# A mixer's turns by DMA, sums in parts, memory rows earlier, and a first weight unit in two

## What is computed

```python
# first block, layer l                      # second block, layer l
x += 0.5*rms_norm(swiglu(rms_norm(x)))      x += rms_norm(parallel_mixer(rms_norm(x)))
x += rms_norm(hybrid_mixer(rms_norm(x)))    x += rms_norm(memory_cross_attention(rms_norm(x), rms_norm(mem)))
x += 0.5*rms_norm(swiglu(rms_norm(x)))      x += rms_norm(swiglu(rms_norm(x)))
```

## Time and profile before

| | |
|---|---|
| median of 3 runs | 2045.92 us (2045.69 to 2047.0) |
| the profiled execution | 2046.49 us, span 2044.6 us |
| TensorE busy | 2022.4 us, 99% |
| VectorE busy | 1411.0 us, 69% |
| ScalarE busy | 1122.0 us, 55% |
| granted TensorE clock, in tenths | 9 (90% or more) in all 40 slices |
| DMA | 389.31 MB, mean 190 GB/s |

### The profile page before, as it was taken

One profiled execution on the slowest core, in us unless ns is written; L12 is line 12 of the kernel. 1 busy time (PEld: TensorE's weight loads), 2 busy tenths in 40 slices (PEclk: granted clock), 3 DMA queues, 4 the chain that ended last, 5 costly groups with the idle time before them and its releaser, 6 DMA issues.

```text
span 2044.6 us, 24517 instructions
## 1 busy us (share of the span) xinstructions
PE 2022.4 (99%) x9754; PEld 1669.8 (82%) x9754; DVE 1411.0 (69%) x1855; ACT 1122.0 (55%) x1414; POOL 0.2 (0%) x4
## 2 busy tenths in 40 slices
PE   7999999999999999999999999999999999999998
PEld 6888887888888888887878888898888888988887
DVE  6656898776667566998776566856756668567565
ACT  5445657564446445667564446656644566565443
POOL 0000000000000000000000000000000000000000
PEclk9999999999999999999999999999999999999999
DMA  8766764557766775664567766444677664446764
GB/s 269 213 209 182 220 202 144 174 192 208 216 205 211 206 216 181 211 191 150 178 212 223 202 189 203 153 150 141 188 209 214 186 201 145 159 140 186 210 212 119
DMA packets 330226, 389.31 MB, mean 190 GB/s; under 512 B 102640, under 2 KB 238464, under 8 KB 330112
## 3 DMA queue, kind: packets, MB, share of 16 engines
q1 hardware_dynamic: 326016, 376.70, 60.7%
q10 hardware_dynamic: 4096, 11.05, 1.5%
HBM read 365.66 MB, written 1.05 MB: 179 GB/s over the span
## 4 chain that ended last, share of the span: by engine, by line
PE 91%; DVE 4%; ACT 2%; DMA 2%; issue 1%; SPq 0%; DVEq 0%; ACTq 0%
PE ps L585 82%; PE ps L1086 2%; DVE w_lo L1827 1%; DMA raw<-in_ffn_w_up 1%; DVE scratch L2092 1%; PE ps L653 1%; ACT w_hi L1249 1%; PE ps L1189 1%; PE ps L1170 1%; PE ps L676 1%; PE ps L822 1%; DVE x L1867 0%; DMA raw<-in_w_in 0%; PE ps L1034 0%; PE ps L728 0%
## 5 line engine op out<-in xcount | busy, mean ns | idle before, releaser
L1827 DVE TENSOR_TENSOR w_lo<-raw,w_hi 128x2048 fp32r<-128x2048 f32 x338 | 772.5, 2289 | 268.1 <-ACT w_hi L1249 265.6
L1249 ACT ACTIVATE w_hi<-raw 128x2048 fp32r<-128x2048 f32 x342 | 648.2, 1898 | 461.5 <-PE ps L585 261.2
L585 PE MATMUL ps<-w_hi,hT_hi 128*128 128x512 f32 x2048 | 807.1, 394 | 2.0 <-DVE w_lo L1827 2.0
L585 PE MATMUL ps<-w_lo,hT_hi 128*128 128x512 f32 x2048 | 798.4, 390 | 0.0
L585 PE MATMUL ps<-w_hi,hT_lo 128*128 128x512 f32 x2048 | 775.4, 390 | 0.0
L585 PEld LDWEIGHTS ps<-w_hi,hT_hi 128*128 128x128 f32 x2048 | 385.0, 188 | 85.9 <-issue 5.5
L585 PEld LDWEIGHTS ps<-w_hi,hT_lo 128*128 128x128 f32 x2048 | 383.6, 188 | 79.8
L585 PEld LDWEIGHTS ps<-w_lo,hT_hi 128*128 128x128 f32 x2048 | 385.3, 188 | 77.1
L585 PE MATMUL ps<-w_hi,bT_hi 128*128 128x512 f32 x592 | 232.3, 392 | 1.6 <-DVE bT_lo L1908 1.5
L585 PE MATMUL ps<-w_hi,bT_lo 128*128 128x512 f32 x592 | 230.5, 389 | 0.0
L585 PE MATMUL ps<-w_lo,bT_hi 128*128 128x512 f32 x592 | 230.5, 389 | 0.0
(11 more groups left out here) (292 smaller groups left out, 1283.3 us busy)
## 6 DMA issues: line engine op xcount, KB each, us to landing
raw<-in_w_in SPq DMA_DIRECT2D x160, 512.0 KB, 4.6
raw<-in_ffn_w_gate SPq DMA_DIRECT2D x88, 512.0 KB, 4.0
raw<-in_ffn_w_up SPq DMA_DIRECT2D x88, 512.0 KB, 5.0
raw<-in_ffn_w_down SPq DMA_DIRECT2D x88, 512.0 KB, 4.3
raw<-in_w_gate SPq DMA_DIRECT2D x44, 512.0 KB, 4.0
raw<-in_w_up SPq DMA_DIRECT2D x44, 512.0 KB, 5.0
raw<-in_w_down SPq DMA_DIRECT2D x44, 512.0 KB, 4.3
raw<-in_w_out SPq DMA_DIRECT2D x32, 512.0 KB, 4.4
```

The lines of the kernel that those rows point to most:

```text
L585: mm = nc.tensor.matmul(bank(t, half), act[:, tiles[i], t * P:(t + 1) * P], w, start=start and (i, n) == steps[0], stop=stop and (i, n) == ...
L1249: nc.scalar.activation(dst, src, ACT.Copy).then_inc(high_ready, 1)
L1827: V.tensor_tensor(lo, src, flat(hi), ALU.subtract).then_inc(low_ready, 1)
```

## The change

- The second mixer's q, k and lru inputs are parted, turned by DMA from SP's queue behind units 9, 10 and 11, and joined; `fox_turn`, `lru_turn` and two copies go, q's factor 1/8 moves into its row scale, `fox_decay` comes after unit 5.
- `sb_sums` takes the softplus rows as a high and a low fp32r part, which VectorE makes; the ones stay in float32. One merge moves ahead of the softplus.
- In `first_pair` the two row turns of x's second half stand together; ScalarE copies the weight unit after the last turned tiles.
- The memory rows are loaded and normalised during the last layer's first feed-forward of the first block, in memory of their own.
- The first unit is loaded, copied and subtracted in two halves; the gains are loaded ahead of the identity and x.

```diff
@@ -299,6 +301,10 @@
     lxy = pairbuf.rearrange("p (t n) -> p t n", t=TT)
+    fq_planes, fq_planes_T = planes(wide[:, 0:1024]), planes_T(rT_f)
+    fk_planes, fk_planes_T = (w.rearrange("p m n -> p (m n)") for w in (vm[:, 0:1, :], vm[:, 1:2, :]))
+    fk_planes, fk_planes_T = planes(fk_planes), planes_T(fk_planes_T)
+    lxy_planes, lxy_planes_T = fq_planes, fq_planes_T
     ry_f, rsq_f = pairbuf[:, 0:512], pairbuf[:, 512:1024]
...
@@ -313,7 +319,8 @@
-    mem_rows, mem_g, mem_sq = merged, conv_y_f, pairbuf
+    mem_rows, mem_g = a_mem(2048).rearrange("p (t n) -> p t n", t=TT), a_mem(1024)
+    mem_sq = out_a
     positions = ctx.enter_context(nc.sbuf_tensor("positions", [P, TT], I32))[:, :]
...
@@ -409,6 +422,11 @@
             u = L.unit(k)
+            if u == 0:
+                for i in range(2):
+                    for dst, src in halves:
+                        sp.dma_start(dst[:, 2 * i:2 * i + 2, :], src[:, 2 * i:2 * i + 2, :]).then_inc(first_landed[i], 16)
+                return
             if u == 1:
...
@@ -529,6 +547,15 @@
                     k += 1
+                    if k == 10:
+                        sp.wait_ge(*after("fox_join", "q_planes", l))
+                        turn_planes(fq_planes_T, fq_planes, fox_q_turned)
+                    if k == 11:
+                        sp.wait_ge(*after("fox_join", "k_planes", l))
+                        turn_planes(fk_planes_T, fk_planes, fox_k_turned)
+                    if k == 12:
+                        sp.wait_ge(*after("lru_turn", "planes", l))
+                        turn_planes(lxy_planes_T, lxy_planes, lru_turned)
                     if (n, kh) == (0, 1):
...
@@ -619,17 +646,18 @@
                         norm_turn(L, j, 0, 1)
-                    if L.sub0 + j and (n, t, i) == (1, 0, 0):
-                        norm_turn(L, j, 1, 0)
+                    if L.sub0 + j and (n, t, i) == (1, 0, 2):
+                        for kh in range(2):
+                            norm_turn(L, j, 1, kh)
                     if n and i == 0:
                         bank_free(t)
+                    if L.sub0 + j == 0 and (n, t, i) == (0, 0, 2):
+                        weights(L, k)
                     pe.wait_ge(hT_hi_ready, L.sub(j, 16, 8 * t + firsts[n] + i + 1))
...
                 def wait(t, i):
-                    if L.sub0 + j and (n, t, i) == (1, 0, 0):
-                        norm_turn(L, j, 1, 1)
                     if i == 0:
...
@@ -639,7 +667,9 @@
             for t, n in order:
-                if t == 0:
+                if t == 0 and L.sub0 + j == 0 and n == 0:
+                    pe.wait_ge(first_low, 1)
+                elif t == 0:
                     weights(L, k + n)
...
@@ -811,16 +841,21 @@
-            pe.wait_ge(*after("sb_keep", f"softplus{c}", l))
+            pe.wait_ge(*after("sb_keep", f"softplus_high{c}", l))
             if c:
...
             for e in range(2):
-                s = sb_sp[:, e * 384:(e + 1) * 384]
-                nc.tensor.matmul(ps[:, 6 + e, 0:384], konst("tri_ge"), s, start=True, stop=False)
-                mm = nc.tensor.matmul(ps[:, 6 + e, P:256], konst("ones"), s[:, 256:384], start=False, stop=True)
+                nc.tensor.matmul(ps[:, 6 + e, 0:384], sb_tri[:, :], sp_hi[:, e * 384:(e + 1) * 384], start=True, stop=False)
+            for e in range(2):
+                nc.tensor.matmul(ps[:, 6 + e, P:256], konst("ones"), sb_sp[:, e * 384 + 256:(e + 1) * 384], start=False,
+                                 stop=False)
+            for e in range(2):
+                pe.wait_ge(*after("sb_keep", f"softplus_low{e}_{c}", l))
+                mm = nc.tensor.matmul(ps[:, 6 + e, 0:384], sb_tri[:, :], sp_lo[:, e * 384:(e + 1) * 384], start=False,
+                                      stop=True)
             mm.then_inc(*done("sb_sums", f"sums{c}"))
...
@@ -967,23 +1002,12 @@
-        def fox_turn(l, which):
-            pe.wait_ge(*after("fox_in", which, l))
-            if which == "k":
-                pe.wait_ge(*after("fox_gate", "rows", l))
-            turn(fq if which == "q" else fk, 4 if which == "q" else 6).then_inc(*done("fox_turned", which))
-
-        def lru_turn(l):
-            pe.wait_ge(*after("lru_in", "xy", l))
-            pe.wait_ge(*after("fox_in", "qT", l))
-            turn(lxy, 4).then_inc(*done("lru_turned", "xy"))
-
         def fox_logits(l, g):
...
             if g == 0:
-                pe.wait_ge(*after("fox_in", "kT", l))
+                pe.wait_ge(*after("fox_join", "k", l))
                 pe.wait_ge(*after("fox_gate", "rows", l))
...
@@ -1094,8 +1118,7 @@
                     ("ret_in", "g"), ("memory_in", "v0"), ("memory_in", "v1")]
-            steps = {(1, 0): [fox_forget], (1, 1): [fox_decay, lambda l: fox_turn(l, "q")],
-                     (2, 1): [lambda l: fox_turn(l, "k")], (3, 1): [lru_turn, lambda l: fox_logits(l, 0)],
+            steps = {(1, 0): [fox_forget], (2, 0): [fox_decay], (3, 1): [lambda l: fox_logits(l, 0)],
                      (4, 1): [lru_gates, lambda l: fox_logits(l, 1)], (5, 0): [lambda l: fox_turn_p(l, 0)],
...
@@ -1242,11 +1265,17 @@
             slot = u % RAW_RING
-            act.wait_ge(raw_landed[slot], (u // RAW_RING + 1) * 32)
+            act.wait_ge(raw_landed[slot], (u // RAW_RING + (slot > 0)) * 32)
             if u >= HIGH_RING:
...
             nc.scalar.activation(dst, src, ACT.Copy).then_inc(high_ready, 1)
+
+        def first_unit_high(i):
+
+            act.wait_ge(first_landed[i], 32)
+            s = slice(1024 * i, 1024 * i + 1024)
+            nc.scalar.activation(w_hi[:, 0, s], raw[:, 0, s], ACT.Copy).then_inc(high_ready if i else first_high, 1)
...
@@ -1319,8 +1348,8 @@
             turned(L, j + 1, 1, 0)
+            turned(L, j + 1, 1, 1)
             high(L, last + PAST)
-            turned(L, j + 1, 1, 1)
...
@@ -1361,7 +1388,11 @@
             for c in range(2, NCHUNK - 1):
+                if memory_here(L, n) and c == 3:
+                    memory_load()
                 chunk(L, k0 + 3 * c - 1, c)
+                if memory_here(L, n) and c == 6:
+                    memory_std(L.l)
             end, c = k0 + U_FFN - 1, NCHUNK - 1
...
@@ -1656,8 +1685,6 @@
             between = {0: lambda: (fox_soft(l), lru_lambda(l)),
-                       2: lambda: (act.wait_ge(*after("fox_turned", "q", l)), copy(fqT, two(4), "fox_in", "qT", 64 ** -0.5)),
-                       3: lambda: (act.wait_ge(*after("fox_turned", "k", l)), copy(fkT, two(6), "fox_in", "kT")),
                        4: lambda: fox_exp(l, 0)}
...
@@ -1676,6 +1703,10 @@
                 dst, stage, step = evicted[n]
+                if n == 0:
+                    act.wait_ge(*after("fox_join", "eighth", l))
+                if n == 4:
+                    act.wait_ge(*after("fox_join", "q", l))
                 rows(dst, chunk_rows(n) if n < 5 else chunk_rows(n)[:, :, 0:256], stage, step)
...
@@ -1773,22 +1804,24 @@
         enter(Layer("A", 0))
-        act.dma_start(const[:, 0:P], d["const"][:, 0:P]).then_inc(ident_loaded, 16)
         rows_of_gains = d["gains"].rearrange("s g (k p) -> (s g k) p", p=P)
-        act.dma_start(x[:, 0, :], d["x"][0, 0:P, :]).then_inc(x_loaded[0], 16)
         for b, (r, end) in enumerate(((0, P), (P, GAIN_ROWS))):
             act.dma_start(gain_rows[0:end - r, b, :], rows_of_gains[r:end, :]).then_inc(gains_loaded, 16)
+        act.dma_start(const[:, 0:P], d["const"][:, 0:P]).then_inc(ident_loaded, 16)
+        act.dma_start(x[:, 0, :], d["x"][0, 0:P, :]).then_inc(x_loaded[0], 16)
         act.dma_start(x[:, 1, :], d["x"][0, P:T, :]).then_inc(x_loaded[1], 16)
...
         act.dma_start(const[:, at:at + width], d["const"][:, at:at + width]).then_inc(const_loaded, 16)
-        high(Layer("A", 0), 0)
+        first_unit_high(0)
         act.wait_ge(gains_ready, 1)
...
                 turned(Layer("A", 0), 0, t, kh)
+                if (t, kh) == (0, 0):
+                    first_unit_high(1)
         for k in range(2, AHEAD + 1):
...
@@ -1825,6 +1858,16 @@
             V.tensor_tensor(lo, src, flat(hi), ALU.subtract).then_inc(low_ready, 1)
+
+        def first_unit_low(i):
+
+            if i:
+                dve.wait_ge(high_ready, 1)
+            else:
+                dve.wait_ge(first_high, 1)
+            s = slice(1024 * i, 1024 * i + 1024)
+            V.tensor_tensor(w_lo[:, 0, s], raw[:, 0, s], flat(w_hi[:, 0, s]), ALU.subtract).then_inc(
+                low_ready if i else first_low, 1)
...
@@ -2127,6 +2173,13 @@
             V.scalar_tensor_tensor(sb_sp, sb_z, 0.0, sb_e, ALU.max, ALU.add).then_inc(*done("sb_keep", f"softplus{c}"))
+            dve.wait_ge(*after("sb_keep", f"softplus{c}", l))
+            V.tensor_copy(sp_hi[:, :], sb_sp).then_inc(*done("sb_keep", f"softplus_high{c}"))
+            dve.wait_ge(*after("sb_keep", f"softplus_high{c}", l))
+            for e in range(2):
+                s = slice(e * 384, (e + 1) * 384)
```

(59 more changed lines are left out.)

15 lines of the change are left out of this document (10 added, 5 removed).

## The result

The changed kernel takes 2033.85 us (median of 6 runs, 2033.39 to 2034.47); the kernel before took 2045.74 us in the runs beside them. The ratio is 0.9943, with an interval of 0.993 to 0.9955: 11.9 us less. The forecast was 2033.0. The sum behind it is less right than the number: one term of it failed by 3.2 us, and others came out larger than predicted.

A forecast was written before the change was run, and what follows sets the result against it. TensorE, busy 99% of the span, was taken to bound the kernel. Terms 5.5 + 3.9 + 0.2 + 1.6 + 2.1 = 13.3 us turned the 2045.92 us median into 2032.6; the forecast was 2033.0, range 2029 to 2040.

The forecast's parts named there:

- second mixer: Turning q, k and lru inputs by DMA takes 48 transposes off TensorE over two layers: net 5.5 us.
- sums in parts: In `sb_sums`, fp32r parts make each call 0.62 us cheaper, call 0 only 0.1: 3.9 us, bounds 2.0 to 4.5.
- merged turns: Two row turns of 4 become one of 8 in 11 places, with no wait there: 0.2 us.
- memory rows: Moving their loads and norm into the first feed-forward gains 1.8 us and costs 0.2 there: net 1.6 us.
- start: Splitting the first unit brings the first product from 14.06 to about 11.6: 2.1 us taken, bounds 0.3 to 3.5.
- The charge of 0.3 us for late joins: Second mixer: k's joined planes might reach TensorE's logits late in the second layer, where the margin was 0 to 1.6 us.
- the credit of 0.6 us to the later `fox_decay`: Second mixer, second layer: moving it one unit (5.45 us) later covers TensorE's 0.6 us wait for VectorE.
- TensorE arrives at 322.93 less what call 0 saved: a wait of 0 to 0.3 us: Sums, calls 1 to 3: VectorE's high part is ready at 322.9, so TensorE hardly waits; 0.62 us gained per call.
- the low parts are ready while TensorE does the high parts and the ones: Sums: VectorE's two low subtracts, 0.45 us each, finish behind TensorE's other matmuls, so they add no wait.
- Rival (a): New waits (copy at 0.96 us in 8 sums, late k planes) and a start of 0.5 us: 2036 to 2041, chance 0.20.
- The open question of the clock: Start: if fast spacing follows the first product as before, 2.4 us is kept; if it stays at 16.8, 1.1 is lost.
- The memory rows' 0.88 us in the feed-forward head: Second feed-forward's start, up to its first down product: 0.88 us of waiting for the normed rows would go.

The follow-up runs named there:

- decay_back: The changed kernel with `fox_decay` back behind unit 4, where it stood before: 2034.09 us.
- x_first: The changed kernel with x's first half issued by SP ahead of the first unit, and the second half's row turns behind the first 4 products: 2032.72 us.
- all_late: The changed kernel with sums 6 products later, x's first half sooner, first norm earlier, and first join ahead of the parts of units 5 and 6: 2030.11 us.

## Why the prediction was right, and where it wasn't

| term | predicted | found |
|---|---|---|
| second mixer | 5.5 | 6.1 between the traces, 6.4 when undone |
| sums in parts | 3.9 (2.0 to 4.5) | 0.7 |
| merged turns | 0.2 | 0.7 |
| memory rows | 1.6 | 2.0, of it 0.91 and 1.1 in the two places |
| start | 2.1 (0.3 to 3.5) | 1.7 |
| sum | 13.3 | 11.2, and 1.25 at the span's end |

**Second mixer: right, with one step wrong.** From the stage's first product to `lru_gates` (L1010 before, L1034 after) it was 64.40 us and is 61.70 in the first layer, 65.22 and 61.70 in the second: 2.70 and 3.52, of which 0.07 each is the merged turns. The 48 transposes count as priced, 5.2 us. The charge of 0.3 us for late joins was not needed: k's planes landed 4.3 to 5.1 us after issue, as the rows said. xy's landed after 6.6 to 8.3 us, outside the 3.2 to 5.1 that I had taken, and only the room behind them hid it. The step that failed is the credit of 0.6 us to the later `fox_decay`: the wait cost 0.9 us and went with the rest of the new mixer, not with that move (decay_back).

**Sums: the term that failed.** Three of its numbers held: 0.17 us for the fp32r matmul (0.175 measured), 0.55 us for the copy (0.56), and softplus and TensorE's arrival as close together as stated. Two steps failed. The first: "TensorE arrives at 322.93 less what call 0 saved: a wait of 0 to 0.3 us" compared two clocks as if they were independent, and the sum then took the wait at nothing (3 x 0.62 in full). They aren't independent: the softplus is released by TensorE's own logits, so all that TensorE saves earlier moves both, and the margin stays what it was, at most 0.5 us. The copy needs 0.57. So the wait came in every call and cost 0.29 us of each, the slower pair behind it included; and call 0, credited with 0.1 us, lost 0.09. The second: "the low parts are ready while TensorE does the high parts and the ones". The second of them is not (it ends at 322.39, TensorE starts the low pair at 322.20), and 0.11 us a call is lost. Rival (a) had this mechanism, a wait in all 8 sums worth 3 us, with the wrong cause (a copy of 0.96 us). It was given 0.20 with its other parts; the loss it priced here, 3 us, was the loss found, 3.2.

**Start.** The first product was to stand at 11.6 and stands at 12.10. The first unit's parts were ready at 7.75, earlier than the 8.2 worked out; x was the bound, as said, but its first half landed at 8.73 instead of the 6.4 of before: the gains, the identity and three of the unit's four loads stood ahead of it (it was issued at 2.14 instead of 1.20). And unit 1, which waits for it, went 2.3 us later than before (8.75 against 6.45). Hence the new wait at 19.31, which I had not named. How much the start gained is known only roughly: the one profile before has 39.02, and the nine after spread from 36.65 to 38.37, so between 0.65 and 2.4 us. The open question of the clock came out between the two answers: the spacing falls from 0.43 to 0.23 us, from the 1.2 to the 2.4 GHz level, at 13.86, 1.8 us after the first product. In x_first it does so at 12.60, 3.5 us after it; before, at 17.17, 3.1 us after it. The granted clock reads 1.00 in all these stretches, so the level is read from the spacing alone. Neither a fixed time nor a fixed delay from the first product fits all three; before that first product TensorE had stood idle for 2.0 us in the kernel before and not at all in the changed one.

**Memory rows and merged turns** were priced from the right rows and came out larger. The memory rows' 0.88 us in the feed-forward head was 1.1. For the merged turns I took only the difference of the turns' own entries (0.44 twice against 0.87, 0.11 us in 11 places, and rounded it up to 0.2) and left out the return from turns to products; the runs give 0.06 a place.

**The sum.** 13.3 us came within 2.1 of what the chain shows, because misses of -3.2 and -0.4 met misses of +0.6, +0.5 and +0.4. The median moved by 11.9 us, 1 us short of the 12.9 forecast from the runs before. That the number came so close is partly luck: the largest miss was a quarter of the whole gain, and the others happened to have the other sign.

## What to carry to other kernels

Before an operation is made cheaper on the bound engine, ask who releases its operand. If that engine itself releases it some steps earlier, the wait is a chain of fixed length, and the gain needs room in the order, not speed: here making a sum 0.57 us cheaper was worth 0.7 us in all, moving it by 6 products 0.7 us, and the two together 5.3. And a step that is moved ahead holds all that is queued behind it for as long as its own operand is late: all_late lost in that way what it had won.

## What the hardware showed that I had not expected

- A pair of fp32r matmuls of 384 columns takes 0.35 us in the chain when TensorE comes to it running, and 0.62 us when it had to wait for its operand; from its start to the next matmul's, 0.35 and 0.46 us.
- In the second mixer a pair of DMA transposes kept its queue for 2.6 us when the queue had been idle before it, and for 3.5 to 6.9 us when weight loads stood just ahead of it; single transposes landed 2.7 to 8.3 us after issue in the changed kernel, 3.2 to 5.1 before.
- The same start code lands its loads differently from run to run: the first product on bT varied by 1.7 us over nine runs, as much as the start part of the change gained between the two profiles, while the 1991 us behind it repeated to 0.2 us.
